# Rotary partners by a shuffle on VectorE instead of products on TensorE, in a two-layer hybrid decoder step

## What is computed

```python
def partial_rope(x, pos):
    half = ROT_DIM // 2
    inv = ROPE_THETA ** (-jnp.arange(half, dtype=jnp.float32) * 2.0 / ROT_DIM)
    ang = pos.astype(jnp.float32)[:, None] * inv[None, :]
    cos = jnp.cos(ang)[:, None, :]
    sin = jnp.sin(ang)[:, None, :]
    xr = x[..., :ROT_DIM].astype(jnp.float32)
    x1, x2 = xr[..., :half], xr[..., half:]
    rot = jnp.concatenate([x1 * cos - x2 * sin, x2 * cos + x1 * sin], axis=-1)
    return jnp.concatenate([rot.astype(x.dtype), x[..., ROT_DIM:]], axis=-1)
```

## Time and profile before

| | us |
|---|---|
| median of 3 runs | 2638.18 |
| lowest and highest | 2637.41, 2643.18 |
| the profiled execution | 2638.53 |
| its span in the trace | 2636.9 |

### The profile page before, as it was taken

How to read it: one execution, slowest core, us unless ns; L and a number is a source line. 1 busy time by engine, 2 the same in 40 slices (tenths; PEclk the granted TensorE clock), 3 DMA queues, 4 the chain that set the end, 5 groups by cost and what they waited for, 6 DMA issues and landing times.

```text
span 2636.9 us, 51469 instructions
## 1 busy us (share of the span) xinstructions
PE 2590.1 (98%) x19408; PEld 2543.3 (96%) x19408; DVE 1496.4 (57%) x2067; ACT 1009.8 (38%) x1377; POOL 351.1 (13%) x299
## 2 busy tenths in 40 slices
PE   8999999999999999999999999999999999999997
PEld 7999889999999999999999999899999999999997
DVE  5466787655554455555545767875555544555555
ACT  5344444433333333333333435443333333333333
POOL 2011112111110011111100111131111100111111
PEclk9999999999999999999999999999999999999998
DMA  6435434445444544544454444344544555454443
GB/s 223 160 130 169 140 132 144 163 165 172 164 166 157 172 154 163 172 164 162 159 165 154 160 138 139 132 151 166 172 163 160 170 165 161 159 173 160 167 160 123
DMA packets 115723, 419.97 MB, mean 159 GB/s; under 512 B 13376, under 2 KB 14656, under 8 KB 115584
## 3 DMA queue, kind: packets, MB, share of 16 engines
q1 hardware_dynamic: 109152, 397.72, 45.2%
q0 software_dynamic: 3472, 14.04, 1.5%
q10 hardware_dynamic: 3024, 7.16, 0.7%
HBM read 411.06 MB, written 11.87 MB: 160 GB/s over the span
## 4 chain that ended last, share of the span: by engine, by line
PE 92%; DVE 5%; ACT 1%; issue 1%; POOL 1%; DMA 0%; DVEq 0%; SPq 0%; ACTq 0%; POOLq 0%
PE gp L1410 29%; PE gp L1412 29%; PE gp L1411 29%; DVE wlo L681 1%; PE mb L1454 1%; DVE qg L932 1%; PE mb L1525 1%; POOL acc L1339 0%; DVE rope_sin L922 0%; PE mb L1514 0%; PE mb L1463 0%; PE mb L1578 0%; PE mb L1570 0%; DVE rstd L706 0%; PE mb L1612 0%
## 5 line engine op out<-in xcount | busy, mean ns | idle before, releaser
L1410 PE MATMUL gp<-xh,whi 128*128 128x288 f32 x4096 | 1226.4, 299 | 14.0 <-DVE xl L1107 10.0
L1411 PE MATMUL gp<-xl,whi 128*128 128x288 f32 x4096 | 1211.2, 296 | 0.0
L1412 PE MATMUL gp<-xh,wlo 128*128 128x288 f32 x4096 | 1207.3, 295 | 0.0
L681 DVE TENSOR_TENSOR wlo<-raw,whi 128x1024 fp32r<-128x1024 f32 x754 | 968.9, 1319 | 342.1 <-ACT whi L402 338.6
L402 ACT ACTIVATE whi<-raw 128x1024 fp32r<-128x1024 f32 x754 | 769.2, 1052 | 595.4 <-PE gp L1412 576.3
L1410 PEld LDWEIGHTS gp<-xh,whi 128*128 128x128 f32 x4096 | 770.5, 188 | 30.5 <-issue 29.1
L1412 PEld LDWEIGHTS gp<-xh,wlo 128*128 128x128 f32 x4096 | 773.9, 189 | 0.0
L1411 PEld LDWEIGHTS gp<-xl,whi 128*128 128x128 f32 x4096 | 771.9, 188 | 0.4
L1410 PE MATMUL gp<-fh,whi 128*128 128x288 f32 x1408 | 416.7, 296 | 0.0
L1411 PE MATMUL gp<-fl,whi 128*128 128x288 f32 x1408 | 415.4, 295 | 0.0
L1412 PE MATMUL gp<-fh,wlo 128*128 128x288 f32 x1408 | 414.0, 294 | 0.0
(11 more groups left out here) (237 smaller groups left out, 1876.3 us busy)
## 6 DMA issues: line engine op xcount, KB each, us to landing
raw<-wstream SPq DMA_DIRECT2D x754, 512.0 KB, 4.1
s<-s_cache POOLq DMA_DIRECT2D x8, 512.0 KB, 9.7
hs_out<-s ACTq DMA_DIRECT2D x8, 512.0 KB, 2.8
caches_out<-caches POOLq DMA_DIRECT2D x8, 496.0 KB, 7.9
x<-x_in ACTq DMA_DIRECT2D x4, 576.0 KB, 9.0
y_out<-x SPq DMA_DIRECT2D x4, 576.0 KB, 2.8
kct<-kt_cache POOLq DMA_DIRECT2D x4, 512.0 KB, 6.3
vct<-v_cache POOLq DMA_DIRECT2D x4, 512.0 KB, 7.9
```

The lines of the kernel that those rows point to most:

```text
L681: v.tensor_tensor(wlo[slot][:], raw[slot][:], whi[slot][:].bitcast(F32), ALU.subtract).then_inc(lo_ready, 1)
L1410: t.matmul(out, w_hi, mv_hi, start=first, stop=False)
L1411: t.matmul(out, w_hi, mv_lo, start=False, stop=False)
L1412: mm = t.matmul(out, w_lo, mv_hi, start=False, stop=last)
```

## The change

It takes the partner products from TensorE. VectorE multiplies the tile itself, out of `pj`, by the sine table, then permutes the result's partitions within each block of 32 with a stream shuffle, in place, and adds the cosine product as before. The matrix `rot` had also given the sign. Now the sign is put into the sine table once, in layer 0, by a column of row sums of `rot` (`rot_sign`) behind the half masks. The tiles are rotated in the order 4, 0, 2, 1, 3: the key first, then the two query tiles of which units 0 and 1 are made. The first three lie in VectorE's first piece, the last two in the second, where before four lay in the first and the key in the second. TensorE's first two pieces are empty, and its first scores wait for `rot2`, the third rotation, instead of `rot4`, the fifth. VectorE waits for `group_out` itself before it reads `pj`. GpSimd's cosine products follow the new order, and its loads of the cached keys and values, like the convolution's first steps, wait for the last rotation of the new order.

```diff
+ROPE_ORDER = (4, 0, 2, 1, 3)
+PARTNER = [(i ^ (ROT_DIM // 2)) if i < ROT_DIM else i for i in range(32)]
...
-        av = Steps(sem("attn_vector"), [s for n in range(5) for s in (f"sin{n}", f"rot{n}")]
+        av = Steps(sem("attn_vector"), [s for n in ROPE_ORDER for s in (f"sin{n}", f"shf{n}", f"rot{n}")]
...
             def half_masks(l):
...
+                if l == 0:
+                    m.then_inc(masks_made, 1)
+                    m = v.tensor_reduce(rot_sign[:], rot, AX.X, ALU.add)
+                    m.then_inc(masks_made, 1)
+                    v.wait_ge(masks_made, 2)
+                    m = v.tensor_scalar(sin, sin, rot_sign[:, 0:1], None, ALU.mult)
                 m.then_inc(masks_made, 1)
-                v.wait_ge(masks_made, l + 1)
+                v.wait_ge(masks_made, l + 3)
...
                 def rope(n):
-                    v.wait_ge(at.sem, at.at(T, f"R{n}"))
-                    v.tensor_tensor(rs_a[:, n % 2, :], mb[n % 4][:, 0:TOK], sin, ALU.mult
-                                    ).then_inc(av.sem, av.step(f"sin{n}"))
+                    k = ROPE_ORDER.index(n)
+                    tile = 4 * gg + Q0 + n if n < 4 else gg + KV
+                    v.tensor_tensor(rs_a[:, k % 2, :], pj[:, tile, :], sin, ALU.mult).then_inc(av.sem, av.step(f"sin{n}"))
                     v.wait_ge(av.sem, av.at(T, f"sin{n}"))
+                    v.stream_shuffle(rs_a[:, k % 2, :], rs_a[:, k % 2, :], PARTNER).then_inc(av.sem, av.step(f"shf{n}"))
+                    v.wait_ge(av.sem, av.at(T, f"shf{n}"))
                     v.wait_ge(ap_.sem, ap_.at(T, f"cos{n}"))
...
-                for n in range(4):
+                v.wait_ge(group_out, attn_in(l))
+                for n in ROPE_ORDER[:3]:
                     rope(n)
                 yield
-                rope(4)
+                for n in ROPE_ORDER[3:]:
+                    rope(n)
```

On GpSimd, in its `attn`:

```diff
-                for n in range(5):
-                    if n >= 2:
-                        e.wait_ge(av.sem, av.at(T, f"rot{n - 2}"))
+                for k, n in enumerate(ROPE_ORDER):
+                    if k >= 2:
+                        e.wait_ge(av.sem, av.at(T, f"rot{ROPE_ORDER[k - 2]}"))
...
-                e.wait_ge(av.sem, av.at(T, "rot4"))
+                e.wait_ge(av.sem, av.at(T, f"rot{ROPE_ORDER[-1]}"))
```

On TensorE, in its `attn`:

```diff
-                    t.wait_ge(av.sem, av.at(T, f"sc{u - 1}" if u else "rot4"))
+                    t.wait_ge(av.sem, av.at(T, f"sc{u - 1}" if u else "rot2"))
...
-                for n in range(4):
-                    partners(n)
-                yield
-                t.wait_ge(av.sem, av.at(T, "sin0"))
-                partners(4)
+                yield
                 yield
                 score(0)
```

More of the change, by code:

```diff
@@ L156, in build @@
         eps = sb("eps", [P, 1])
+        rot_sign = sb("rot_sign", [P, 1])
         half_mask = {i: sb(f"half_mask{i}", [P, P // (2 * HALVES[i])]) for i in MASKED}
@@ L329, in build @@
                                         "pT3", "ah3", "sst", "ses", "pts", "sah"])
-        ap_ = Steps(sem("attn_gpsimd"), [f"cos{n}" for n in range(5)] + ["vst", "qs", "stored"])
-        at = Steps(sem("attn_tensor"), [f"R{n}" for n in range(5)]
-                   + ["sc0", "tv", "sc1", "pt0", "pv0", "sc2", "pt1", "pv1", "sc3", "pt2", "pv2", "pt3", "pv3"]
+        ap_ = Steps(sem("attn_gpsimd"), [f"cos{n}" for n in ROPE_ORDER] + ["vst", "qs", "stored"])
+        at = Steps(sem("attn_tensor"), ["sc0", "tv", "sc1", "pt0", "pv0", "sc2", "pt1", "pv1", "sc3", "pt2", "pv2", "pt3", "pv3"]
                    + ["st", "ss", "pts", "pvs"])
@@ L874, in conv @@
                     yield
-                v.wait_ge(at.sem, at.at(T * 2 + 1, "R4"))
+                v.wait_ge(av.sem, av.at(T * 2 + 1, f"rot{ROPE_ORDER[-1]}"))
                 v.wait_ge(ap_.sem, ap_.at(T * 2 + 1, "vst"))
@@ L919, in rope @@
                 def rope(n):
-                    v.wait_ge(at.sem, at.at(T, f"R{n}"))
-                    v.tensor_tensor(rs_a[:, n % 2, :], mb[n % 4][:, 0:TOK], sin, ALU.mult
-                                    ).then_inc(av.sem, av.step(f"sin{n}"))
+                    k = ROPE_ORDER.index(n)
+                    tile = 4 * gg + Q0 + n if n < 4 else gg + KV
+                    v.tensor_tensor(rs_a[:, k % 2, :], pj[:, tile, :], sin, ALU.mult).then_inc(av.sem, av.step(f"sin{n}"))
                     v.wait_ge(av.sem, av.at(T, f"sin{n}"))
+                    v.stream_shuffle(rs_a[:, k % 2, :], rs_a[:, k % 2, :], PARTNER).then_inc(av.sem, av.step(f"shf{n}"))
+                    v.wait_ge(av.sem, av.at(T, f"shf{n}"))
                     v.wait_ge(ap_.sem, ap_.at(T, f"cos{n}"))
                     if n == 4:
-                        v.tensor_tensor(krg[:], rs_a[:, 0, :], rt_a[:, 0, :], ALU.add).then_inc(av.sem, av.step("rot4"))
+                        v.tensor_tensor(krg[:], rs_a[:, k % 2, :], rt_a[:, k % 2, :], ALU.add
+                                        ).then_inc(av.sem, av.step("rot4"))
                         return
@@ L931, in rope @@
                         src = slice(64 * half, 64 * half + 64)
-                        m = v.tensor_tensor(qg[dst:dst + 64, 2 * (n % 2) + half, :], rs_a[src, n % 2, :],
-                                            rt_a[src, n % 2, :], ALU.add)
+                        m = v.tensor_tensor(qg[dst:dst + 64, 2 * (n % 2) + half, :], rs_a[src, k % 2, :],
+                                            rt_a[src, k % 2, :], ALU.add)
                     m.then_inc(av.sem, av.step(f"rot{n}"))
```

4 lines of the change are left out of this document (2 added, 2 removed).

## The result

The changed kernel takes a median of 2649.75 us (2647.51 to 2652.42, 6 runs); the kernel before took 2637.89 us in the runs beside it (2637.41 to 2643.18, 6 runs). The ratio is 1.0044, with a 95% interval of 1.0031 to 1.0056. On a second chip, where the kernel before had a median of 2640.77 us, it took 2650.16 us (2647.87 to 2652.02, 7 runs), a ratio of 1.0029, 1.0017 to 1.0040. So the kernel is slower by 0.3 to 0.4%; the medians lie 11.9 and 9.4 us apart. The prediction said slower and 2645.0 us; both medians lie in its range, near the upper end.

The account below looks back on a forecast made before the run. VectorE's queue was taken to bound the attention groups: 0.9 + 2.4 = 3.3 us a layer, +6.6 us for two. 2638.5 + 6.6 − 0.3 is 2644.8, given as 2645.0 us, range 2639.5 to 2650.5.

Parts of the forecast that it names:

- The bound: In the two attention groups of each layer, VectorE's queue sets the pace; TensorE waits for the key and `al`.
- The shuffle: Twenty added VectorE shuffles of 128x288, taken as 0.46 us each, bounded by 303 ns and 518 ns.
- Contention: VectorE beside GpSimd in each rotary block: 0.1 us added to each of three sine products, 0.36 us to the split.
- L: VectorE's lateness at the end of each rotary block: 11.37 us against 8.98 us, so 2.4 us.
- First group, L - 1.5: First group of each layer: TensorE's slack of 1.5 us before the first unit's probabilities absorbs part, leaving +0.9 us.
- Second group, L in full: Second group of each layer: VectorE's queue ends in the wait at `al`, so the whole +2.4 us goes through.
- At no cost: Layer 0's sign edit, about 0.9 us, hides in VectorE's 1.81 us idle; GpSimd's cache loads, some 2.5 us later, cost nothing.
- The clock: After new waits of 1.7 to 2.6 us TensorE may drop to 1.2 GHz; one such stretch costs 1.7 us.
- the sum of 2644.8: Whole run: profiled 2638.5 us plus 6.6 for both layers, less 0.3 from profile to median.
- base of 2638.2: The median of the kernel before's runs, 0.3 us below its profiled execution, from which the forecast started.
- The likeliest case: The sum as worked out, +6.6 us over two layers, given 58%.
- Rival 3: Two to four more stretches at TensorE's lower clock, behind places where a delay stays, give 2650 us; 13%.
- The waits for the weight split: First groups: the fifth weight slab's split follows the rotations, now L later; TensorE, early by up to 3.4 us, waits there.

Follow-up runs that it names:

- e4: The changed kernel with a second, identity shuffle behind each first, result unchanged; 2660.5 us, ratio 1.0079 to the kernel before.
- e9: The kernel of e2 without its twenty TensorE partner products, VectorE's instructions untouched; 2640.14 us, ratio 0.9992 to the kernel before.
- e5: The changed kernel with the sign already in the loaded sine table, its two VectorE instructions removed; 2649.99 us, ratio 1.0039 to the kernel before.
- e2: The kernel before with only the new rotation order, partner products kept on TensorE, no shuffle; 2635.61 us, ratio 0.9987 to the kernel before.
- e7: The kernel of e2 with the sums of the last two query rotations moved from VectorE to GpSimd; 2636.34 us, ratio 0.9984 to the kernel before.
- e10: The kernel of e7 run again on a second chip; 2635.16 us, ratio 0.9981 to the kernel before.
- e6: The changed kernel without GpSimd's cosine products, the sum taking the unmultiplied head instead; 2643.49 us, ratio 1.0006 to the kernel before.

## Why the prediction was right, point by point

- **The bound.** Right. Both waits that were read as VectorE's were its queue: e4 adds 2.6 us to each block and moves the turns by 10.4 in all, e9 removes all the products and gets next to nothing.
- **The shuffle.** 0.48 us for 128x288, taken as 0.46 with bounds of 0.303 and 0.518. The yardstick of an instruction with both inputs in SBUF was good, the copy's was not. The Trainium skill, VectorE: DVE Perf Modes, section The perf-mode tier table, knows a shuffle in the slowest mode only; the trace agrees by these 0.48 us, which are below the 0.57 estimated from that page.
- **Contention.** The mechanism was right, its size and places were not. Forecast were 0.1 us on each of three sine products and 0.36 on the split. Measured: 0.60 on each of two sine products (1.06 and 1.05 against 0.45), nothing on the split (1.22), and pairs of sums of 0.92 us, 0.11 below the 1.03 that had been taken for them. The step that failed is to read the sums' growth from 1.03 to 1.24 as a share. The pair of 1.03 us was not alone either: GpSimd's two products run until 277.62, beyond its start at 277.36. It ends at 278.39, 0.77 us behind them, and the pair of 1.24 us ends 0.78 us behind its cosine product (280.16 and 279.38), so already these rows read as a queue, with 0.92 us for a pair alone. So do the rows of after: GpSimd's two cosine products end at 277.26, and the sine product begun at 276.51 ends at 277.57, 0.3 us behind them, so it worked mostly once they were through. Then a split holds from 282.43 to 283.65, the cosine product begun at 282.58 ends at 284.31, about 0.7 us later, and the sine product begun at 283.57 ends at 284.62, 0.3 us behind that. The Trainium skill, SBUF — State Buffer, section SBUF: two separate sides, says this for a VectorE instruction with two SBUF inputs beside a GpSimd one that reads SBUF: whichever starts first has the shared pair for its whole instruction and the other is blocked. The trace agrees but for 0.14 us: the sine product ends 0.31 us, not 0.45, behind GpSimd's. Priced in this way, a sine product costs up to 0.8 us more each time it starts behind a cosine product of 0.81 us. That the errors nearly cancel, L = 2.6 against 2.4, is luck.
- **First group, L - 1.5.** Forecast +0.9, with L = 2.6 it would be +1.1; measured +1.2. The slack of 1.5 us was real, less 0.15 us that pass between the end of the probabilities and the turn (295.36 and 295.51 in after), which makes up the difference.
- **Second group, L in full.** Forecast +2.4, measured +2.6, with a wait of 2.60 us at `al` as before.
- **At no cost.** Right for the sign edit (e5). The later cache loads show no wait of their own.
- **The clock, and the level of the kernel before.** This term was mis-sized. The profiled execution has three more half-speed stretches than before, 5.2 us more lost, but by what the turns leave over only 1.3 us of its 9.0 are due to anything but the queue. Of the 11.9 us between the first medians the turns leave 4.2, and 2.5 of these lie in the kernel before: its six runs there have a median of 2637.9 us, its 75 later ones a mean of 2640.4. The 13 runs of the changed kernel average 2649.8 us, 9.4 above that, 1.7 more than the queue's 7.7. So the way from the sum of 2644.8 to 2649.8 us is 1.1 us of queue, 2.2 us by which the base of 2638.2 was low (the profile behind it had a clock of 0.993, the 75 runs have 0.9919), and 1.7 us that go with the lower clock of the changed kernel; this last is a remainder and not measured by itself.
- **The cases.** The likeliest case had the clock at zero. Rival 3, the sum with two to four more half-speed stretches, named 2650 us at 13 in 100, and the measurement fell there. That it did so within 0.3 us is partly luck, since 2.2 us of it are the low base, which no case had.
- **The waits for the weight split.** The prediction foresaw one in each first group; they are 1.92 us each. Not foreseen were those of 2.65 and 2.63 us in the second groups. These four are 9.1 of the 13.3 us; the other eight are 0.4 to 0.8 us each, like the five of before. They aren't lost time of their own; they are the first place at which the late block is met.

Left open is what makes a given wait end in a half-speed stretch. In after, the wait of 2.60 us at 398.54 is followed by a clock of 1.00, that of 2.65 us at 362.99 by one of 0.52. Over all runs the lower clock goes with more waiting in e9 against e2 (0.9901 and 0.9925) and in e4 against the changed kernel (0.9883 and 0.9904), but e7 and e10, with a shorter wait at `al` than e2 (2.1 against 2.6 us), have 0.9911, and 9 and 7 half-speed stretches against 5. So waiting alone does not explain it.

## What to carry to other kernels

Before work is moved off the busiest engine, see in each place which engine's queue ends the wait there: here 9.6 us of products on an engine that is busy 98% were worth under 2 us by the turns and at equal clock, and 2.6 us a block on one that is busy 57% cost 7.7. An operand that moves from PSUM to SBUF changes who it collides with; price the whole of the other engine's instruction, not a share. Where a kernel's time goes with the granted clock, compare runs of equal clock before a tenth of a per cent is put down to an edit, and take the base of a forecast from more than three runs.

## What the runs showed of the hardware

- A shuffle of 128x288 fp32 inside blocks of 32 partitions takes 0.48 us, and loading its mask 0.01 us, each time, at once in front of it. Beside a cosine product it keeps its 0.48 to 0.49 us.
- A VectorE product with both inputs in SBUF takes 0.45 us alone and 1.05 us when GpSimd's cosine product is still running, itself held up by a split; behind a split without a cosine product it takes 0.45 (e6). It ends 0.3 us behind GpSimd's product. With one input in PSUM it stays at 0.44 to 0.46 us beside the same cosine product. A sum on GpSimd with 64x288 takes 0.80 us, where VectorE needs 0.46.
- One more thousandth of granted clock over the run goes with 1.6 to 3.1 us less, and runs of the same kernel differ by three thousandths (before) to five (e2).
